# Shared expert and router of a MoE step: weights stationary, products reordered, a place of its own for the last down weights

## The reference

```
h      = rms_norm(x, g)                          # 520 x 1024
scores = sigmoid(h @ w_r)                        # 64 experts
eidx, w = 8 experts per token, from the best 4 of 8 groups; w scaled to sum 2.5
y  = sum over the token's experts of  w * (silu(h @ w_gate[e]) * (h @ w_up[e])) @ w_down[e]
y += (silu(h @ s_gate) * (h @ s_up)) @ s_down    # the shared expert, 256 wide
out = rms_norm(x + y, g_final)
```

## Time and profile before

| | us |
|---|---|
| median of 3 runs (lowest to highest) | 1163.1 (1159.67 to 1173.99) |
| the profiled execution | 1160.63 |
| its span in the profile | 1158.9 |
| TensorE busy in the span | 1085.3 (94%) |
| VectorE busy | 740.9 (64%) |
| ScalarE busy | 641.5 (55%) |

### The profile page before, as it was taken

One profiled execution on the slowest core, in us unless ns is written; L12 is line 12 of the kernel. 1 busy time (PEld: TensorE's weight loads), 2 busy tenths in 40 slices (PEclk: granted clock), 3 DMA queues, 4 the chain that ended last, 5 costly groups with the idle time before them and its releaser, 6 DMA issues.

```text
span 1158.9 us, 17553 instructions
## 1 busy us (share of the span) xinstructions
PE 1085.3 (94%) x5968; PEld 810.0 (70%) x5968; DVE 740.9 (64%) x1322; ACT 641.5 (55%) x848; POOL 265.4 (23%) x180
## 2 busy tenths in 40 slices
PE   6999999898879998999999999999999999999981
PEld 5998459897449886566666666666666666666661
DVE  5734625533834344288888888888877877778852
ACT  4383423333633121267777777777776666766663
POOL 1003210000000100233333333333333333333320
PEclk8999999899989789999999999999999999999995
DMA  9403405332991512399999999999999999999935
GB/s 309 194 1 115 153 35 219 139 152 87 350 327 49 218 75 109 109 335 361 357 365 361 364 362 356 360 365 362 369 366 357 351 361 367 372 368 363 344 96 165
DMA packets 65494, 303.25 MB, mean 262 GB/s; under 512 B 12711, under 2 KB 15347, under 8 KB 40870
## 3 DMA queue, kind: packets, MB, share of 16 engines
q1 hardware_dynamic: 50254, 266.15, 60.4%
q0 software_dynamic: 15200, 36.55, 12.9%
HBM read 285.53 MB, written 34.04 MB: 276 GB/s over the span
## 4 chain that ended last, share of the span: by engine, by line
PE 79%; DMA 12%; DVE 5%; ACT 2%; issue 1%; SPq 1%; DVEq 0%; POOLq 0%; ACTq 0%
PE pair L1780 20%; PE pair L176 17%; PE pair L1812 14%; PE pair L1793 9%; DMA regC<-in_exp_w_up 8%; PE pair L1567 5%; PE pair L1765 4%; PE pair L1470 3%; DMA regA<-q_rows 2%; PE pair L1725 2%; PE pair L1692 1%; DMA regB<-in_xa_wo 1%; DVE regL L1080 1%; DMA regA<-in_w_in 1%; PE pair L1800 1%
## 5 line engine op out<-in xcount | busy, mean ns | idle before, releaser
L1780 PE MATMUL pair<-w_hi,h_parts 128*96 128x512 f32 x768 | 267.7, 430 | 0.0
L705 POOL DMA_INDIRECT acc_rows<-regL x64 | 94.5, 1476 | 396.5 <-ACT regL L1002 213.0
L1812 PE MATMUL pair<-w_hi,act_parts 128*96 128x512 f32 x512 | 165.6, 405 | 8.1 <-DVE act_parts L1417 7.9
L1780 PEld LDWEIGHTS pair<-w_hi,h_parts 128*96 128x96 f32 x768 | 121.5, 165 | 69.7 <-issue 33.9
L696 POOL DMA_INDIRECT regL<-h_rows,regL x65 | 140.8, 2167 | 102.7 <-DVE regL L1287 75.3
L176 PE MATMUL pair<-h_hi,w_parts 128*128 128x260 f32 x640 | 132.0, 288 | 3.8 <-DVE h_lo L1074 3.5
L1002 ACT ACTIVATE regL<-pair,regL 96x1024 f32<-96x1024 f32 x64 | 71.0, 1110 | 113.4 <-PE pair L1812 113.4
L1379 DVE TENSOR_TENSOR lo_A<-regA,w_hi 128x1536 fp32r<-128x1536 f32 x64 | 111.8, 1748 | 0.0
L957 ACT CAST w_hi<-regA 128x1536 fp32r<-128x1536 f32 x64 | 94.6, 1481 | 30.1 <-DMA regA<-in_exp_w_up 23.7
L176 PEld LDWEIGHTS pair<-h_hi,w_parts 128*128 128x128 f32 x640 | 105.3, 193 | 4.8 <-issue 3.0
L1812 PEld LDWEIGHTS pair<-w_hi,act_parts 128*96 128x96 f32 x512 | 80.1, 166 | 37.4 <-issue 5.6
(11 more groups left out here) (322 smaller groups left out, 2096.1 us busy)
## 6 DMA issues: line engine op xcount, KB each, us to landing
regA<-in_exp_w_gate SPq DMA_DIRECT2D x32, 1024.0 KB, 11.0
regA<-in_exp_w_up SPq DMA_DIRECT2D x32, 1024.0 KB, 21.6
regA<-in_exp_w_down SPq DMA_DIRECT2D x32, 1024.0 KB, 23.6
regB<-in_exp_w_down SPq DMA_DIRECT2D x32, 1024.0 KB, 23.7
regB<-in_exp_w_gate SPq DMA_DIRECT2D x16, 1024.0 KB, 11.6
regB<-in_exp_w_up SPq DMA_DIRECT2D x16, 1024.0 KB, 22.8
regC<-in_exp_w_gate SPq DMA_DIRECT2D x16, 1024.0 KB, 10.6
regC<-in_exp_w_up SPq DMA_DIRECT2D x16, 1024.0 KB, 24.0
```

The source lines that it names most:

```text
L705: pool.indirect_dma_start(acc_rows, bass.IndirectOffsetOnAxis(ap=kept[0:SLOTS, r, 0:1].bitcast(U32), axis=0), yX[r][0:SLOTS, :], None, bou ...
L1780: ins = pe.matmul(out, x, w, start=False, stop=half == 1 and k == CUT_K - 1 and s == 2, skip_group_check=True)
L1812: ins = pe.matmul(pair[2][0:SLOTS, h, :], act_parts[:, x, k, :], w[:, k, cols], start=k == 0 and s == 0, stop=k == KF - 1 and s == 2)
```

## The change

- The router's weights are stationary and 256 or 264 tokens stream by, in two halves of the output's partitions (experts of half 0 on 0 to 63, of half 1 on 64 to 127). ScalarE takes the sigmoid into `sT`; three transposes, `rs`, turn it, and ScalarE copies it to `sco`. VectorE copies tile 0 of `hR`.
- TensorE's order becomes `sg` 0, `su` 0, `pos`, `sg` 1, `tab`, `su` 1.
- The shared down has features on partitions: for each of 8 tiles of features 12 products in the split form. Its weights are cut by ScalarE and VectorE (`sdw_hi` lies in the ring's fourth place of down weights), its activation too (`shared_parts`). VectorE adds each result to `xT`. After the turn of block 0, TensorE turns `xT` into rows, `sr`, which ScalarE copies and POOL stores as before.
- SP loads the ring's fourth down weights when the last `sd` is made; VectorE's cuts of block 0's gate and up weights move between the adds.
- The high part of the last block's down weights has a place of its own, `last_hi`, and is cut ahead of down 62's copy.

The diff without its unchanged lines:

```diff
+QUARTER = SEQ // 2
...
-    o += [("rt", "act")]
-    o += [(("hR", t), "act") for t in range(NTT)]
-    for m in range(KF):
-        o += [(("sg", m), "act"), (("su", m), "dve")]
-    o += [("pos", "dve", 2, 0), (("sd", 0), "act", 2, 1), (("sd", 1), "act", 2, 2), ("tab", "dve", 2, 0)]
-    o += [(("sd", 2), "act", 2, 1), (("sd", 3), "act", 2, 2), (("sd", 4), "act", 2, 2)]
+    o += [("rt", "act"), (("hR", 0), "dve"), ("rs", "act")]
+    o += [(("hR", t), "act") for t in range(1, NTT)]
+    o += [(("sg", 0), "act"), (("su", 0), "dve"), ("pos", "dve"), (("sg", 1), "act"), ("tab", "dve"), (("su", 1), "dve")]
+    o += [(("sd", m), "dve", 2, (m + 1) % 3) for m in range(KD)]
+    o += [(("sr", t), "act", 2, 2 - 2 * (t % 2)) for t in range(NTT)]
...
-        with nc.sbuf_tensor("lo_C", [P, 4096], F32R) as lo_C:
+        with nc.sbuf_tensor("lo_C", [P, 6144], F32R) as lo_C:
...
+            pass
+        with nc.sbuf_tensor("unused_L5", [P, 10872], F32), nc.sbuf_tensor("shared_parts", [P, 2, KF, NT], F32R) as shared_parts:
...
+        sT = view(regL, 11896, QUARTER + DEC)
...
+        last_hi = view(w_hi, 5120, KF, D)
+        sdw_hi, sdw_lo = WD_lo[3], view(lo_C, 4096, KF, D)
...
+        sdw_cut, sdw_left, sa_hi, sa_lo = sem("sdw_cut"), sem("sdw_left"), sem("sa_hi"), sem("sa_lo")
...
+            sp.wait_ge(made, J.no[("sd", KD - 1)] + 1)
...
-            sp.wait_ge(made, J.no[("sd", NTT - 1)] + 1)
+            sp.wait_ge(made, J.no[("sr", NTT - 1)] + 1)
...
-                J.wait_taken(pool, ("sd", t))
+                J.wait_taken(pool, ("sr", t))
...
+            a.wait_ge(sh_in, 48)
+            a.copy(sdw_hi, sdw).then_inc(sdw_cut, 1)
-            a.activation(sco[:, 0:TT, :], pair[p][:, 0, 0:TT * NE].rearrange("p (t e) -> p t e", t=TT), ACT.Sigmoid)
-            J.take(a.activation(sco[0:DEC, TT, :], pair[p][0:DEC, 0, TT * NE:NTT * NE], ACT.Sigmoid), "rt")
-            for t, (t0, n) in enumerate(TILES):
+            a.activation(sT[0:NE, 0:QUARTER], pair[p][0:NE, 0, 0:QUARTER], ACT.Sigmoid)
+            J.take(a.activation(sT[NE:2 * NE, :], pair[p][NE:2 * NE, 0, 0:QUARTER + DEC], ACT.Sigmoid), "rt")
+            def take_rows(t):
+                n = TILES[t][1]
+            p = J.wait_made(a, "rs")
+            a.copy(sco[:, 0:TT, :].rearrange("p (h i) e -> p i h e", h=2),
+                   pair[p][:, 0, 0:2 * P].rearrange("p (i h e) -> p i h e", i=2, h=2))
+            J.take(a.copy(sco[0:DEC, TT, :], pair[p][0:DEC, 0, 2 * P + NE:2 * P + 2 * NE]), "rs")
+            for t in range(1, NTT):
+                take_rows(t)
+                J.wait_taken(a, ("su", m))
+                a.copy(shared_parts[:, 0, m, :], sA[:, m, :]).then_inc(sa_hi, 1)
...
-            a.wait_ge(made, J.no[("su", KF - 1)] + 1)
...
-                p = J.wait_made(a, ("sd", t))
-                J.take(a.copy(rows[0:n, t, :].rearrange("p (h n) -> p h n", h=2), pair[p][0:n, :, :]), ("sd", t))
-            for t in range(NTT):
-                start_sums(t)
+                p = J.wait_made(a, ("sr", t))
+                J.take(a.copy(rows[0:n, t, :].rearrange("p (h n) -> p h n", h=2), pair[p][0:n, :, :]), ("sr", t))
...
-            def cut_down(r, b, landed):
+            def cut_down(r, b, landed, hi=WD_hi):
-                a.copy(WD_hi, WD[r]).then_inc(wd_hi, 1)
+                a.copy(hi, WD[r]).then_inc(wd_hi, 1)
...
+            for t in range(NTT):
+                start_sums(t)
...
+            cut_down(RING - 1, last, n_turns, last_hi)
-            cut_down(RING - 1, last, n_turns)
...
+            v.memset(sT[0:NE, QUARTER:QUARTER + DEC], 0.0)
...
-            J.wait_taken(v, "rt")
+            p = J.wait_made(v, ("hR", 0))
+            J.take(v.tensor_copy(rows[:, 0, :].rearrange("p (h n) -> p h n", h=2), pair[p][:, :, :]), ("hR", 0))
+            J.wait_taken(v, "rs")
...
-            for m in range(KF):
+            v.wait_ge(sdw_cut, 1)
+            v.tensor_tensor(sdw_lo, sdw, sdw_hi.bitcast(F32), ALU.subtract).then_inc(sdw_left, 1)
+            def shared_act(m):
+            def shared_leave(m):
+                v.wait_ge(sa_hi, m + 1)
+                v.tensor_tensor(shared_parts[:, 1, m, :], sA[:, m, :], shared_parts[:, 0, m, :].bitcast(F32),
+                                ALU.subtract).then_inc(sa_lo, 1)
+            shared_act(0)
...
+            shared_leave(0)
...
-            for half in range(2):
-                cut_up(0, 0, half)
...
-            for t in range(2):
-                slots(t, t)
-                onehot_(t + 1)
+            shared_act(1)
+            shared_leave(1)
+            slots(0, 0)
+            onehot_(1)
+            def shared_added(m):
+                p = J.wait_made(v, ("sd", m))
+                J.take(v.tensor_tensor(halves(xT[:, m, :]), halves(xT[:, m, :]), pair[p][:, :, 0:HALF], ALU.add), ("sd", m))
+            shared_added(0)
+            shared_added(1)
+            slots(1, 1)
+            onehot_(2)
+            shared_added(2)
+            shared_added(3)
+            cut_up(0, 0, 0)
+            shared_added(4)
+            shared_added(5)
+            cut_up(0, 0, 1)
+            shared_added(6)
+            shared_added(7)
...
-            def cut_down(r, b):
+            def cut_down(r, b, hi=WD_hi):
-                v.tensor_tensor(WD_lo[r], WD[r], WD_hi.bitcast(F32), ALU.subtract).then_inc(wd_lo, 1)
+                v.tensor_tensor(WD_lo[r], WD[r], hi.bitcast(F32), ALU.subtract).then_inc(wd_lo, 1)
...
-            cut_down(RING - 1, last)
+            cut_down(RING - 1, last, last_hi)
...
-            for t, (t0, n) in enumerate(TILES):
-                for k in range(KD):
-                    ready(k)
-                    ins = pe.matmul(pair[p][0:n, 0, t * NE:(t + 1) * NE], hT[:, k, t0:t0 + n], rw[:, k, :], start=k == 0, stop=k == KD - 1)
+            for k in range(KD):
+                ready(k)
+                for half, n in enumerate((QUARTER, QUARTER + DEC)):
+                    ins = pe.matmul(pair[p][half * NE:(half + 1) * NE, 0, 0:n], rw[:, k, :],
+                                    hT[:, k, half * QUARTER:half * QUARTER + n], start=k == 0, stop=k == KD - 1)
...
+            rows_of(("hR", 0), hT, *TILES[0])
+            p = J.begin(pe, "rs")
+            J.wait_taken(pe, "rt")
+            for i in range(3):
+                n = P if i < 2 else DEC
+                ins = pe.transpose(pair[p][0:n, 0, i * P:(i + 1) * P], sT[:, i * P:i * P + n], ident[:, :])
+            J.made_by(ins)
-                rows_of(("hR", t), hT, t0, n)
+                if t:
+                    rows_of(("hR", t), hT, t0, n)
+            def shared_up(what, w, m):
+                project((what, m), lambda k: w[:, k, m * P:(m + 1) * P], lambda k: hT[:, k, :], range(KD))
-            for m in range(KF):
-                project(("sg", m), lambda k: sgw[:, k, m * P:(m + 1) * P], lambda k: hT[:, k, :], range(KD))
-                project(("su", m), lambda k: suw[:, k, m * P:(m + 1) * P], lambda k: hT[:, k, :], range(KD))
+            shared_up("sg", sgw, 0)
+            shared_up("su", suw, 0)
...
-            def shared_down(t):
-                t0, n = TILES[t]
-                p = J.begin(pe, ("sd", t))
-                for m in range(KF):
-                    J.wait_taken(pe, ("su", m))
-                    for h in range(2):
-                        pe.matmul(pair[p][0:n, h, :], sA[:, m, t0:t0 + n], sdw[:, m, h * 512:(h + 1) * 512],
-                                  start=m == 0, stop=False, skip_group_check=True)
-                for k in range(KD):
-                    ins = pe.matmul(pair[p][0:n, k // 4, (k % 4) * P:(k % 4 + 1) * P], xT[:, k, t0:t0 + n], ident[:, :],
-                                    start=False, stop=k % 4 == 3, skip_group_check=True)
-                J.made_by(ins)
-            shared_down(0)
-            shared_down(1)
+            shared_up("sg", sgw, 1)
+            shared_up("su", suw, 1)
...
+            def shared_down(*ms):
+                places = [J.begin(pe, ("sd", m)) for m in ms]
+                for kf in range(KF):
+                    pe.wait_ge(sa_lo, kf + 1)
+                    for m, p in zip(ms, places):
+                        cols = slice(m * P, (m + 1) * P)
+                        for h in range(2):
+                            of = slice(h * HALF, (h + 1) * HALF)
+                            for i, (w, x) in enumerate(((sdw_hi, 0), (sdw_lo, 0), (sdw_hi, 1))):
+                                ins = pe.matmul(pair[p][:, h, 0:HALF], w[:, kf, cols], shared_parts[:, x, kf, of],
+                                                start=kf == 0 and i == 0, stop=kf == KF - 1 and i == 2)
+                        if kf == KF - 1:
+                            J.made_by(ins)
+            pe.wait_ge(row_table, 1)
+            n_turns = turns(pe)
-            shared_down(2)
+            pe.wait_ge(sdw_left, 1)
+            shared_down(0, 1)
-            shared_down(3)
-            shared_down(4)
-            pe.wait_ge(row_table, 1)
```

(20 more changed lines are left out.)

## The result

The changed kernel took 1125.95 us (median; 1123.88 to 1127.35), beside 1168.16 for the kernel before in the same job: ratio 0.964, 95% interval 0.957 to 0.972. These medians are 42 us apart because two of the four runs before took over 1173. Repeated later for the spread of its runs the changed kernel took 1130.55 (1123.82 to 1133.08; ratio 0.970, 0.965 to 0.976). The profiled execution took 1127.35 us, its span 1125.6 instead of 1158.9: 33.3 us less, where the sum said 30.5. A run more than 1.5% longer than the fastest of its kernel counts as disturbed and is left out of the comparisons.

A forecast was written before the change was run, and what follows sets the result against it. TensorE was taken as the limit for 79% of the span. Gains of 25.0 us before block 0 and 5.5 at the end, 30.5 from 1160.6, gave 1130.1 (1132.6 from the median); forecast 1131.5, range 1126 to 1137.

The forecast's parts named there:

- the sum: Whole kernel: 25.0 us from block 0 starting earlier plus 5.5 at the end, 30.5 against the profiled 1160.6 us.
- Router: Router products: 16 with column halves side by side, first 4.9 us at 1.2 GHz, ending at 399.9 instead of 411.32, gain 11.4.
- Routing and places: Router to up 1: routing starts at 402.3, places' product runs 419.5 to 423.9, up 1 ends at 438.1 without waiting.
- Shared down: Up 1 to block 0: VectorE's adds, then transposes, take 21.1 us; block 0 at 459.2 instead of 484.35, gain 25.1.
- lower bound in the prediction: Shared down: if TensorE alone set the pace, 19.1 us behind up 1, which would give 2 more.
- Clock at the hand-over: Hand-over, almost only transposes from about 451.6 to 459.2: full clock as at the kernel's start, so nothing added.
- The end: Block 63: earlier cut, last product 2.79 us instead of 5.17, scatter 63 waits for 62's; gain 5.5, between 3.8 and 6.1.
- POOL's start sums: Before the loop: POOL's stores come at about 457 to 460, as shortly before it as they did; costed at nothing.
- The loop: Loop over 64 blocks of experts: rounds unchanged, so no gain or loss was counted.
- Rival 3: Expert loop: transfers, not TensorE, set the pace; all 16 rounds at 42.64 us, 43 us more, 1174; chance 0.06.

The follow-up runs named there:

- runs with light transfers: Gathers and scatter-adds cut to 8 of a block's 96 rows, in both kernels: 1155.82 us for the kernel before, 1123.93 us for the changed kernel.

## Why the prediction was right, step by step

- **Router: right.** 5.70 us (5.34 in the repeat) for 5.9 predicted, halves side by side, the clock rising within the stage, as the windows show. The low clock was priced at 4.9 us of the stage and took 3.9; over eight profiles it took 3.2 to 6.0. That the total came within 0.2 us is in part luck.
- **Routing and places: right.** VectorE's routing starts 7.9 us behind the router's start (405.21) for 8.3, the places' product 24.9 for 25.5, and up 1 ends 43.5 behind for 44.1. The 0.6 us are mostly the router's 0.2 and the turns of the rows, 3.71 for the 4.2 predicted: the 0.13 us of a turn came from 411.32 to 416.55, whose first us lay at the clock of 0.50.
- **Shared down: mechanism right, term mis-sized by 1.4 us.** Block 0 starts 19.7 us behind up 1's end; 21.1 was predicted. VectorE's adds were priced at 0.7 each, but two in a row take 1.21 us of the chain, and the two slots with their one-hots take 3.3 us for 3.8; so the add of feature 6, for which the turn of block 0 waits, ends at 454.0 and the last one 13.8 behind up 1, not 15.1. TensorE's last product of the shared down ends at 453.84 by the timeline, and from 441.65 on its products stand with hardly a gap: both engines arrive together. The lower bound in the prediction (TensorE alone, 19.1) was the nearer one.
- **Clock at the hand-over: right, on a ground that does not bear it.** It is 1.00 in the window and in 320 further transposes. The prediction rested it on the kernel's start, where the transposes ran at the low level's pace for most of the stretch; what held is that transposes keep the full level, for which the prediction had no row. So this step was luck in part.
- **The end: right**, 5.3 us for 5.5, with the scatter of 62 as what limits it, as predicted.
- **POOL's start sums: a term put at nothing that cost 1.0 us.** The prediction had them come as shortly before the loop as they did; the gather behind them starts 4.3 us later relative to block 0, and TensorE waits for it.
- **The loop: the term set to zero was not zero in the profiles** (-4.2, with that 1.0 inside). Rival 3 named the mechanism, transfers that set the pace, and took it for a danger to the new kernel. It was in the old one's time: the runs with light transfers are 7.3 us shorter than the full kernel before (1155.8 against 1163.1 in that job), of which the profiles show 2.2 at the end and the rest in the loop. The new kernel likely has the same loss in some of its executions. Of the 5.5 us by which the first job's median lies below the forecast, the hand-over's terms explain about 2; the rest is likely this loss, absent there and present in the second job, which lies 1 us below. None of the longer runs of the changed kernel was profiled, so this is not shown.

## What to carry to other kernels

Where one engine's chain has no gaps, a removed product gives about its whole duration (here 10.6 and 11.6 us of router gave 9.5 and 12.1), and a wait can be filled by moving independent work of the same engine over it; the value of such a move depends on how much other cover is left, so single undoings don't add up. Check a reading of the clock against the spacing of the records: a column that says 1.00 may stand for a stretch without a record. Look at the time from issue to landing of each round's loads, not only at stalls: a loop may look bound by TensorE while its loads fall behind by a us or two a round. Compare two kernels in such a loop by the stages that the change touches, and let the medians only confirm it.

## What the runs showed of the hardware that was not expected

- The old router, 80 records of 64 columns with hT as weights, is 17.31 us long at a granted clock of 0.50 in both kernels although TensorE is busy all the time; the new one begins at 0.50 as well, and the clock rises 3.2 to 6.0 us into it.
- With fp32 transposes alone TensorE keeps the full level (35 us at 1.00) and also comes up to it: in the changed kernel's start their spacing falls from 0.213 to 0.109 us at 8.70, with nothing else on TensorE before.
- The loads fall behind at different speed in executions of the same program, with a DMA share of about 1.0 in all: after 400 us of loop the up weights land 21.1 us behind their issue in one profile, 9.3 in another.
- A second queue may be close to setting the pace. A scatter starts only when the last has landed; at the end of the changed kernel it is 0.85 us from landing to the next start (1105.04 to 1105.89). In the loop scatters land 8.7 us behind their issue, which by the same addition is 9.6 of the 9.97 us that TensorE needs for a block (an estimate). No run here tests it.
